# Attention of a hybrid layer: where VectorE applies the gate and takes the key maxima, behind the first block of row maxima instead of the second

## What is computed

```python
def fox_block(q, k, v, c_q, c_k, q_pos, k_pos):
    s = jnp.einsum('bqhd,bkhd->bhqk', q, k) * ATTN_SCALE
    s = s + swap(c_q)[:, :, :, None] - swap(c_k)[:, :, None, :]
    s = jnp.where(k_pos[None, :] <= q_pos[:, None], s, -jnp.inf)
    p = jax.nn.softmax(s, axis=-1)
    return jnp.einsum('bhqk,bkhd->bqhd', p, v)

# per layer: 4 heads of 64, queries in blocks of 128 rows, block i sees keys 0 .. 128*(i+1)
mixed_a = o_a * jax.nn.silu(g_a)
```

## Time and profile before

| | us |
|---|---|
| median of 3 runs | 1602.19 |
| lowest and highest | 1600.78, 1603.14 |
| the profiled execution's own time | 1604.0 |
| its span in the trace | 1602.2 |
| TensorE busy | 1538.6 (96%) |
| VectorE busy | 958.4 (60%) |
| ScalarE busy | 636.5 (40%) |

### The profile page before, as it was taken

The page is one execution under the profiler, slowest core; times in us unless marked ns, Lnnn a source line. Parts: engine busy times, 40 slices in busy tenths (PEclk is TensorE's granted clock), DMA queues, the critical chain, the costliest instruction groups (busy, mean ns, idle before and its releaser), DMA issues.

```text
span 1602.2 us, 35979 instructions
## 1 busy us (share of the span) xinstructions
PE 1538.6 (96%) x14428; PEld 1142.3 (71%) x14428; DVE 958.4 (60%) x2300; ACT 636.5 (40%) x1307; POOL 82.1 (5%) x99
## 2 busy tenths in 40 slices
PE   6999999999999999999989999989898999999998
PEld 5787788888888888888656666678777854444443
DVE  5688846786367666587786656445454458333333
ACT  3246443554345531355655655623323371100011
POOL 1010000000000000000000000000000004222220
PEclk9999999999999999999999999999999999999999
DMA  6366483447534564355897566577656289999893
GB/s 231 124 212 202 173 276 134 163 151 257 169 134 151 196 216 132 106 165 179 282 302 219 177 201 183 170 232 230 191 175 210 92 314 335 358 350 354 326 335 123
DMA packets 184512, 341.72 MB, mean 213 GB/s; under 512 B 22229, under 2 KB 124117, under 8 KB 173654
## 3 DMA queue, kind: packets, MB, share of 16 engines
q1 hardware_dynamic: 166826, 256.32, 49.1%
q0 software_dynamic: 10496, 72.98, 12.2%
q10 hardware_dynamic: 7024, 10.12, 1.7%
HBM read 286.13 MB, written 55.35 MB: 213 GB/s over the span
## 4 chain that ended last, share of the span: by engine, by line
PE 83%; DVE 5%; ACT 5%; DMA 3%; issue 2%; SPq 1%; ACTq 0%; DVEq 0%
PE psum L1073 32%; PE psum L1360 25%; PE psum L1060 7%; PE psum L1046 5%; PE psum L1320 4%; PE psum L1235 3%; PE psum L1306 3%; PE psum L1665 2%; ACT big L1750 1%; PE psum L1119 1%; ACT L1750 1%; DVE big L2368 1%; PE psum L1568 1%; SPq L845 1%; DMA out_shiftP<-big 1%
## 5 line engine op out<-in xcount | busy, mean ns | idle before, releaser
L1073 PE MATMUL psum<-big 128*128 128x256 f32 (+1 forms) x1920 | 433.3, 383 | 0.6 <-ACT zst L1763 0.6
L1073 PEld LDWEIGHTS psum<-big 128*128 128x128 f32 x1920 | 364.4, 190 | 57.7 <-issue 2.0
L1360 PE MATMUL psum<-big 64*64 64x64 f32 (+4 forms) x5440 | 258.9, 272 | 16.2 <-issue 10.1
L1763 ACT ACTIVATE zst<-psum 128x256 f32<-128x256 f32 (+1 forms) x336 | 126.9, 385 | 351.4 <-PE psum L1073 342.9
L1360 PEld LDWEIGHTS psum<-big 64*64 64x64 f32 (+2 forms) x5440 | 179.7, 133 | 101.1 <-issue 74.8
L1073 PE MATMUL psum<-big,wbuf 128*128 128x256 f32 (+1 forms) x768 | 182.9, 386 | 1.9 <-ACT zst L1763 1.8
L1073 PEld LDWEIGHTS psum<-big,wbuf 128*128 128x128 f32 x768 | 146.0, 191 | 27.4 <-issue 5.2
L2368 DVE SCALAR_TENSOR_TENSOR big<-big,pars 128x512 f32<-128x512 f32 x240 | 161.0, 745 | 0.4
L1007 POOL DMA_INDIRECT big<-in_cache_v,pidx x64 | 68.2, 1065 | 639.7 <-PE psum L1320 426.0
L1046 PE MATMUL psum<-ident,big 128*128 128x128 f32 (+2 forms) x558 | 79.5, 281 | 8.7 <-ACT big L2035 3.3
L1750 ACT ACT_TABLE_LOAD x61 | 78.3, 1283 | 13.5 <-DMA big<-in_x_first 7.7
(11 more groups left out here) (333 smaller groups left out, 2027.7 us busy)
## 6 DMA issues: line engine op xcount, KB each, us to landing
big<-in_k_pages SPq DMA_DIRECT2D x432, 128.0 KB, 2.3
big<-wS SPq DMA_DIRECT2D x36, 768.0 KB, 5.8
zst<-in_k_pages SPq DMA_DIRECT2D x80, 128.0 KB, 2.8
wS<-big SPq DMA_DIRECT2D x12, 768.0 KB, 5.8
wbuf<-in_w_pairs SPq DMA_DIRECT2D x18, 512.0 KB, 3.9
big<-in_w_pairs SPq DMA_DIRECT2D x18, 512.0 KB, 4.5
zT<-big ACTq DMA_DIRECT2D x16, 512.0 KB, 3.3
rwS<-big SPq DMA_DIRECT2D x32, 256.0 KB, 4.3
```

The source lines that it names most:

```text
L1073: last = nc.tensor.matmul(psum[:, bank, 0:wide(p) // 2], left(k), right(k), start=first and k == 0, stop=k == 3, skip_group_check=True)
L1360: return nc.tensor.matmul(out, l, r, start=start, stop=stop, skip_group_check=True)
L1763: nc.scalar.activation(parts_[:, U % 2, COPIED_TO[j], 0:n], psum[:, (0, 1, 2, 0, 1, 2, 3)[j], 0:n], ACT.Copy, scale=0.125 if i == U_QA els ...
```

## The change

`finish(j-1)` and `early_scores(j-1)` are called behind the row maxima of block 0 of item j+1, for every item. Before, they were called behind block 1 where the item has more than one block, and behind block 0 where it has one.

```diff
                     for c in range(blocks(j + 1)):
                         row_max(j + 1, c)
-                        if j >= 1 and c == min(1, blocks(j + 1) - 1):
+                        if j >= 1 and c == 0:
                             finish(j - 1)
                             early_scores(j - 1)
                     negate(j + 1)
```

## The result

| | us | ratio to before, 95% interval |
|---|---|---|
| before, median of 8 runs | 1601.49 (1596.09 to 1603.98) | |
| changed kernel, median of 8 runs | 1608.96 (1601.26 to 1611.54) | 1.0044 [1.0030, 1.0058] |
| changed kernel again, 12 executions | 1605.60 (1597.53 to 1616.18) | 1.0034 [1.0010, 1.0059] |

The changed kernel is slower, by 7.0 us by the first ratio and 5.4 us by the second, where +3.0 was forecast. The first median is outside the range that was forecast, the second, 1605.60, inside it; both ratios are on the other side of the line at 0.2%. The sign of the sum was right, its size was not.

What follows compares the result with a forecast made beforehand. TensorE was taken as the bound in items of three and four blocks, with full DMA engines from 820 to 840. 3.81 - 0.78 - 0 = +3.0 us gave 1605.2 us, range 1602.3 to 1607.6.

Steps and rivals of the forecast that it cites:

- The stall: Items 24 to 31: block 3 waits for block 1's later-read banks, 0.51 us each, 4.1 us on TensorE.
- Nothing elsewhere: Items 8 to 23 have no block 3; later `nb` in three-block items and ScalarE's exponentials were to cost nothing.
- E: End of item 29's closing transpose, in item 31; block 3 was to start at E + 2.27, without a wait E + 1.76.
- 3.81: Delay in us of item 31's `nb` and the next stage's start: seven stalls, 3.57, plus 0.24 in item 31.
- The gain of 0.78 us: Item 14's key step no longer waits for the gate of item 13; bounds 0 and 0.78 us.
- a gain of 0.9 us and a loss of 1: Bounds for item 10's key step, starting about 0.9 us sooner ahead of item 12's wait for pages; counted at 0.
- rival E: Attention's end: the stalls end in the 1.78 us wait as next-stage inputs come in time; +1.5 us, 1603.7, chance 0.05.
- B: Item 12's pages follow their earlier issue, so item 10's key step gives 0.9 us too; +2.1, 1604.3, chance 0.12.
- C: Earlier copy of the keys takes DMA engines from item 12's pages; +3.2 and more, at 0.9 us 1606.1, chance 0.15.
- D: Eight short TensorE waits let its clock fall from 2.4 to 1.2 GHz; one fall gives +4.7, 1606.9, chance 0.03.
- a start of item 12's step more than 0.3 us off 839.2: Sign at item 12's key step that would show the forecast wrong.

Runs made afterwards that it cites:

- The kernel with the gate alone: Against the kernel before: only the gate goes behind block 0 in all items, the key maxima stay behind block 1; 1.0014 [0.9997, 1.0031].
- four-block: Against the kernel before: the change in items 24 to 31 alone; 1.0033 [1.0015, 1.0051].
- three-block: Against the kernel before: the change in items 16 to 23 alone; 0.9996 [0.9977, 1.0015].
- added-matmul: The kernel before with block 2's second-head matmul done twice in each of items 24 to 31; 1.0044 [1.0025, 1.0063].

## Why the prediction was wrong

The sum was +3.0 us, and 5.4 to 7.0 were measured. Two terms of it failed. The stall was priced at its wait alone, 0.51 us, and costs 0.61: 4.85 us on TensorE instead of 4.1. And item 9, under "Nothing elsewhere", loses about 0.3 us. Together they are about 1 us of a miss of 2.4 to 4.0. About 1.5 us more go with a lower clock, which no term of the sum had, and the rest stays open.

**The stall: right in place and mechanism, mis-sized by a fifth.** All of the working's instants hold in item 31. E is 1027.11 + 0.33 = 1027.44. The gate was to start at E + 0.04 and did (1027.47); block 1 at E + 0.91, 1028.34 measured against 1028.35; block 3 at E + 2.27 = 1029.71, exactly. Without a wait it would have started 0.96 behind block 2, at 1029.20, so the wait is the forecast 0.51. The step that failed is the next one, "TensorE waits 0.51 us that it doesn't wait now", taken as the whole loss. Behind the wait, block 3 takes 1.06 us from its start to the next transposes (1029.71 to 1030.77), where in a running row it takes 0.96. The eight matmuls of rows 4, two heads side by side, taken one pair at a time from narrow windows of the kernel before, show where the difference sits (pair one and two are block 2, three and four block 3):

```profile
1025.93 0.70 PE L1235 MATMUL psum<-big 64*128 64x512 f32 x2
1026.46 0.59 PE L1235 MATMUL psum<-big 64*128 64x512 f32 x2
1026.89 0.60 PE L1235 MATMUL psum<-big 64*128 64x512 f32 x2
1027.32 0.59 PE L1235 MATMUL psum<-big 64*128 64x512 f32 x2
```

From the first pair to the second it is 0.53 us, from then on 0.43. Block 3 alone starts a row of its own behind its wait, and takes 0.53 there too (1029.71 to 1030.24). So the 0.10 us isn't a price of waiting: block 2 pays it without a wait, and block 3 pays it once the row is broken in two. 0.51 + 0.10 is the measured 0.61 to 0.62. The kernel with the gate alone agrees: 0.51 - 0.34 + 0.10 = 0.27, measured 0.26. On TensorE this makes 4.85 us where 4.1 was forecast, and ahead of item 31's `nb` 7 x 0.61 + 0.24 = 4.5 in place of 3.81, the upper bound that I had set; from closing 22 it came 99.16 us later where it was 94.68.

**The gain of 0.78 us: met, but it isn't seen in the interval.** Item 14's step starts at 852.01, right behind the transposes, and the piece from item 12's pages to closing 14 is 0.77 us shorter wherever the gate of item 13 is moved as in the changed kernel, save where the clock falls in it. The middle interval behind it stays at 74.67, so nothing there takes it back. What hides it is the piece ahead, which I had set at nothing between a gain of 0.9 us and a loss of 1. Item 10's step does start 0.84 us sooner behind closing 9 (1.43 or 1.44 us in place of 2.28, in every kernel that moves its gate). Then comes the wait for item 12's pages. From closing 9 to the second half of item 12's step it took 17.55 to 22.46 us in the six kernels that move the gate item 10's step waits for and leave all transfers in their places (mean 19.8), and 18.19 to 21.93 in the seven with that gate in its old place (mean 19.4). So 0 was right on the mean, with an error of about a microsecond, but single executions lie up to 3 us off it.

I had also read the 1.89 us at 839.21 wrongly, as a wait for pages alone. Four other kernels with the old order (the repeat of before, and the four-block, three-block and added-matmul kernels) show 0.87 us at the same step, and with the pages there 5 us early it still shows 0.87: that much is the gate of item 11, and about 1.0 us is pages. A wait for two things is put down to the one that came last, and the length in the bracket hides that the other would have held the engine nearly as long. So three gate waits go (0.84, 0.87 and 0.70 us). The two ahead of the pages bring TensorE to them earlier and are waited away there on the mean; the one behind them is kept. The first interval as a whole shows no difference above its scatter: with all transfers in their places it took 50.22, 54.26, 51.05, 50.64 and 55.78 us in the five kernels with the gates of the two-block items moved (mean 52.4), and 53.62, 51.95, 52.38, 51.79 and 51.67 in the five with the old order there (mean 52.3). A gain of 0.78 us is within that error.

**"Nothing elsewhere": right for three blocks, wrong by 0.3 us for two.** The three-block change alone gave 0.9996 and left its interval at 74.67. But I looked for late exponentials at 980 only, in items of three and four blocks. In item 9 `nb` comes later, as the gate ahead of block 1 waits for the transpose, and TensorE, which has little work there, waits for the exponentials: 5.60 to 5.90 us on the mean, as above. The rows of L1750 and the interval agree; no kernel took this item alone, and the old order itself ranges over 0.44 us, so the 0.3 us is a difference of means.

**The next stage.** From closing 22 to its start it is 115.81, 115.83 and 115.92 us in the three kernels whose four-block items are changed, and 111.08 to 113.11 (mean 112.0) in twelve that leave them. So on the mean it moves by 3.9 us, not by TensorE's 4.85: about a microsecond of the last wait is eaten up, the part of rival E that came true. This last wait scatters, though, from 0.78 to 2.8 us in the twelve, and is 0.66 to 0.77 in the three; against the shortest of the twelve it moves by 4.7 to 4.8 us and next to nothing is eaten up. The forecast for this instant, 3.81, is met by luck, by a stall that was set too small and an absorption that wasn't in the sum.

**The rivals.** B (the pages follow the issue, so that item 10's 0.9 us count too) isn't borne out: the piece up to item 12's pages isn't shorter on the mean. C (the copy of the keys) isn't borne out as I put it: the waits are long in the kernel that moves a gate and not the copy, and short in the one that moves the copy. That is one profile each of something that scatters; with the copy brought forward by a whole item, several times its lead here, the time was 1.0006 [0.9989, 1.0023], so a loss under 1 us isn't excluded. That TensorE arrives earlier and so waits longer fits the rows, but no experiment holds the pages' arrival still. D (the clock falls from the eight short waits) falls: over the whole stretch of the stalls the clock stayed at 1.00 in the changed kernel (columns of the earlier trace rows).

```profile
935.00:1045.00 110.00, 106.99 (x1096) 67.76 (x1096) 59.98 (x234) 62.17 (x100) 0.00 (x0) 1.00 0.58 170
```

The Trainium skill (TensorE: Matmul & The Clock Gate, section A second HAM failure mode: psum-queue depth-cycling) warned of such gaps; waits of this size and distance did not do it here. E (the stalls end in the wait of 1.78 us) is right for at most about 1 us of 4.85 on the mean, and wrong for the rest. Of the signs that I had set, a start of item 12's step more than 0.3 us off 839.2 was none: the kernel before has it at 838.21 in its second profile. And the range's lower end, 1603.7 less 1.5, is 1602.2 and not 1602.3; nothing hangs on it.

**What stays open.** The corrected sum is 3.9 us to the next stage's start (up to 4.8 by the shortest waits there), less 0.77 for item 14, and about 0.3 in item 9: 3.4 to 4.3 us, or 0.21 to 0.27%, with a microsecond of error from item 12's pages. The four-block part alone measured 0.33% and holds its share of this, 3.9 us or 0.24%, in its interval; the whole change measured 0.34% and 0.44%, and the interval of the latter begins at 0.30%. So 1 to 4 us of the result have no place in the attention that I could point to.

Part of that goes with the clock. Over the 163 executions of the kernel before, the time falls by 1.5 us for each 0.001 of mean granted clock. The changed kernel's 20 executions took 6.0 us more than these on the mean, at a clock of 0.9901 against 0.9911: 1.5 us of the 6.0 go with the clock, and **4.5 us** are left, with an error of 0.8. The corrected sum lies at the lower side of that. The four-block part alone, whose clock was 0.9915, comes out at 5.3 us by the same reckoning.

Where the lower clock comes from is shown in part. In the profiles of kernels whose wait at item 12's pages was 2.3 us or more in one piece, the clock fell behind it in five and stayed in one (2.95 us). Four of these five are among the ten kernels that move the gate item 10's step waits for, one among the other ten. Over all their executions the ten have a mean clock of 0.9904 (116 executions) and the others of the experiments, which leave that gate, 0.9909 (108), with errors of 0.0002 each. So the earlier gates seem to bring some falls of the clock, worth under 1 us. But the kernel with only the two-block items moved has a mean clock of 0.9907, and the one with all but the four-block items moved 0.9897 and 1.0025. I can't say why these differ, and chance isn't excluded.

## What to carry to other kernels

Where a consumer releases a buffer later, price the producer's stall from the release and add what the first instruction of a row costs more than the following ones, since the stall breaks one row into two; here that extra was a fifth of the wait, in every item. Before counting a gain, look for the next wait on the same engine that a transfer sets: here two gains ahead of it were lost in it on the mean, and the one behind it was kept to 0.01 us. When two things come late together, read the length that the lesser one would have alone from a kernel in which the greater is out of the way. Compare intervals between fixed instructions rather than spans, on an engine whose marks the change doesn't move itself: here the slower kernel had the shorter profile, and one set of marks was biased. If an interval scatters, cut it at the wait that scatters; the rest may repeat.

## What the runs showed of the hardware

- Two heads' products of 64 rows each, which TensorE keeps side by side (they start within 0.01 us of each other), take 0.96 us a block in a row of two blocks; one head's product added alone took 0.86 us, nearly as much as both together.
- The first pair of 512-column matmuls in a row takes 0.53 us to the next, a following one 0.43, whether there was a wait ahead of the row or not. A wait that breaks a row of two blocks in two costs its length and 0.10 us.
- The same 16 pages, issued at the same place, can be waited for 0.17 or 2.92 us. When copies of 1040 KB were moved away from them, the waits showed up where they went: 4.4 to 6.2 us in one interval, for nothing that could be measured in the other. In one of the long waits the DMA engines were at 0.60 and not full.
- Over 163 executions of one kernel, 0.001 of mean granted clock goes with 1.5 us of 1600.
